# Feed-forward entry: the norm's root moved from the input of three weight units to their outputs

## The chip, the cores and the metric

The kernel runs on one core of a Trainium2 chip. Its metric is the device time in microseconds (us) of one execution; a profile gives in addition the span from the first to the last recorded instruction. Five engines work from queues of their own: TensorE (PE; PEld is its weight load), VectorE (DVE), ScalarE (ACT), GpSimd (POOL) and SyncE (SP, which issues DMAs). Each engine runs its own instructions in the order of the program, and they are tied together by semaphores: an instruction may wait until a counter has reached a value, and raise one when it ends.

## The reference

The reference is a block of two layers on 256 tokens of width 1024, all in float32: a mixer with mixture of experts, and then a second mixer with a feed-forward part. The change lies where the second mixer ends and the feed-forward begins:

```python
for l in range(DEPTH):                      # DEPTH is 1
    u = rmsnorm(h, norm_mix_w[l])
    h = h + hybrid_mixer_2(u, ...)          # ends with merged @ w_o
    v = rmsnorm(h, norm_ffn_w[l])
    h = h + conv_gated_mlp(v, ...)
return rmsnorm(h, final_norm_w)

def rmsnorm(x, w):
    y = x * rsqrt(mean(x * x, axis=-1, keepdims=True) + EPS)
    return y * w

def conv_gated_mlp(v, w_up, ffn_conv_w, ffn_conv_b, w_down):
    h1, h3 = split(v @ w_up, 2, axis=-1)    # w_up is 1024 x 5632
    h1 = causal_dwconv(h1, ffn_conv_w) + ffn_conv_b   # 3 taps along the tokens
    return (silu(h1) * h3) @ w_down
```

The root, rsqrt of a token's mean square, is one number for a token. It multiplies the whole row of the token, so it can be applied to v or to v @ w_up. The convolution mixes tokens, so it has to be in before the taps.

## The kernel before, in words

Tokens stand in two row groups of 128 (t = 0, 1), the width of 1024 in eight groups of 128 (k = 0 to 7). Products in float32 are made of three passes of a shorter float format: each operand is split in a high part (a copy on ScalarE) and a low part (a difference on VectorE), and `product3` issues high by high, high by low and low by high.

The back of the kernel is one stream of weight units through a ring of three slots (`Stream`). SP loads a unit of 1 MB; ScalarE makes its high part (`hi`, line 112, function `split_hi` around it), VectorE its low part (`lo`, line 116, `split_lo`), PE multiplies. A load waits for the low part of the unit three earlier, a high part for the products of the unit three earlier. The second mixer has units 0 to 55, the feed-forward (`ffn`, `BASE` 56) 22 units of up-projection and 12 of down-projection. I call the feed-forward's units 0, 1, 2, ...; the split of unit 57 is that of the feed-forward's unit 1.

The mixer's last four units (52 to 55) multiply the merged rows by `w_o`, two for each half of 512 columns, into banks 4 to 7. VectorE adds them to the hidden rows `s.h` (line 1987, four additions: half c, row group t), each raising `h_done`; between them it makes low parts of units 56 and 57. 

The feed-forward begins with the norm. ScalarE loads the table for logarithm and exponential (line 2222), squares each half of each row group (line 2185), and when the second half of a row group is squared it makes the root (lines 234, 236) and a diagonal matrix of it, `diag` (line 2228). PE multiplies the rows by the diagonal with the rows as its fixed operand (line 2318, 16 products of 128x128, two instructions each), which turns and scales them in one step, into banks 3 to 6. ScalarE copies the turned rows out with the norm's weight as scale (line 2231: `v_hi`), VectorE makes the low parts (line 2266: `v_lo`), and PE starts the first unit as the low parts arrive, k by k.

A unit of the up-projection is 48 products of 128x256 (`features_out`, lines 168 to 170): two feature groups of 128, eight k, three passes, into one of banks 0 to 2. For units 0 to 10 (the convolved half) ScalarE makes the newest tap with the bias (line 2238), then the high part of the unit three later, then Silu (line 2242); VectorE makes the two older taps of both feature groups (line 2276, four instructions), which frees the bank, then the low part of the unit three later. Units 11 to 21 are multiplied by the result.

Of the kernel before, what the change touches and what calls it, by code (L numbers as in the profile page):

```python
# [9 lines left out]
FP32 = mybir.dt.float32  # L10
# [6 lines left out]
P = 128  # L17
T = 256
# [1534 lines left out]
def mixer2(nc, A, s):  # L1553

    XBC_TAPS, A_TAPS, N_HEADS, N_GROUPS = 4, 3, 32, 4
    with ExitStack() as ctx:
# [271 lines left out]
        def vector(dve):  # L1828
# [151 lines left out]
            for c in range(2):  # L1980
                for t in range(TT):
                    if t == 0:
                        dve.wait_ge(out_first, c + 1)
                    else:
                        dve.wait_ge(st.gemm_done, 52 + 2 * c + 2)
                    hc = s.h[:, t, 512 * c:512 * c + 512]
                    dve.tensor_tensor(hc, hc, s.bank[4 + 2 * c + t][:, :], ALU.add).then_inc(h_done, 1)
                split_lo(dve, 56 + c)

        def tensor(pe):  # L1990

# [127 lines left out]
            for n in range(52, 56):  # L2119
                c, kh = O_OUT[n - 52]  # L2120
                pe.wait_ge(st.lo_done, n + 1)
                rows_out(pe, s.bank[4 + 2 * c:6 + 2 * c], st.w(n % 3, 4, 512), 4, lambda part, k: merged_part(part, 4 * kh + k),
                         kh == 0, kh == 1, out_first, st.gemm_done)

        return Programs(sync, gpsimd, scalar, vector, tensor)


def ffn(nc, A, s):
# [5 lines left out]
    with ExitStack() as ctx:  # L2134
# [5 lines left out]
        def sem(name):  # L2140
# [15 lines left out]
            "fw_loaded", "summed", "r_ready", "diag_ready", "vt_mm", "vt_hi", "vt_lo", "tap_done", "h1_ready", "p_ready",  # L2156
            "p_hi_done", "out_first", "act_own", "dve_own", "weighted", "out_ready", "stored"))
        last_scaled = sem("m4_last_scaled")
        h1_flat = h1[:, :, :].rearrange("p a t -> p (a t)")
        squares_of_h = (prod[:, 0, :, :].rearrange("p a t -> p (a t)"), h1_flat[:, 2048:2560])  # L2160
        result = h1_flat[:, 0:2048].rearrange("p (t d) -> p t d", t=TT)
# [17 lines left out]

        def half(x, t, c):  # L2180
            return x[:, t, 512 * c:512 * c + 512]

        def square_half(act, own, i, t, c, done):
            act.wait_ge(done, 2 * c + t + 1)
# [34 lines left out]
        def scalar(act):  # L2219
            own = Count(act, act_own)  # L2220

            act.preload_act_table_set(LOG_EXP)
            for c in range(2):
                for t in range(TT):
                    square_half(act, own, 0, t, c, s.h_done)
                    if c:
                        root_of(act, own, 0, t)
                        act.activation(diag[:, t, :], C("identity"), ACT.Copy, scale=mv[:, t, 4:5]).then_inc(diag_ready, 1)
            for k in range(KD):
                act.wait_ge(vt_mm, k // 2 + 1)  # L2230
                act.activation(v_hi[:, k, :], s.bank[3 + k // 2][:, T * (k % 2):T * (k % 2) + T], ACT.Copy, scale=s.col("norm_ffn_w_2", k)).then_inc(vt_hi, 1)
            split_hi(act, 2)
            for n in range(UP_UNITS):
                act.wait_ge(st.gemm_done, BASE + n + 1)
                if n < UP_UNITS // 2:
                    for t in range(2):
                        f = 2 * n + t
                        act.activation(h1[:, f, :], s.bank[n % 3][:, T * t:T * t + T], ACT.Identity,
                                       scale=s.col("ffn_conv_w_2", KF * (TAPS - 1) + f), bias=s.col("ffn_conv_b_2", f)).then_inc(tap_done, 1)
                    split_hi(act, n + 3)  # L2240
                    act.wait_ge(evac_sem[n % 3], n // 3 + 1)
                    act.activation(pair(h1, n), pair(h1, n), ACT.Silu).then_inc(h1_ready, 1)
                else:
                    c = n - UP_UNITS // 2
                    split_hi(act, n + 3)
                    act.wait_ge(p_ready, c + 1)
                    act.activation(pair(p_hi, c), prod[:, c % 2, :, :].rearrange("p a t -> p (a t)"), ACT.Copy).then_inc(p_hi_done, 1)
            for n in range(UP_UNITS, N_UNITS):
                split_hi(act, n + 3)
            act.preload_act_table_set(LOG_EXP)  # L2250
            for c in range(2):
                for t in range(TT):
                    square_half(act, own, 1, t, c, summed)
                    if c:
                        root_of(act, own, 1, t)
                        act.wait_ge(weighted, 2 * c + t + 1)
                        if t == 0:
                            act.activation(result[:, 0, :], result[:, 0, :], ACT.Copy, scale=mv[:, TT, 4:5]).then_inc(out_ready, 1)
                        else:
                            act.activation(half(result, 1, 1), half(result, 1, 1), ACT.Copy, scale=mv[:, TT + 1, 4:5]).then_inc(out_ready, 1)  # L2260

        def vector(dve):
            own = Count(dve, dve_own)
            for k in range(KD):
                dve.wait_ge(vt_hi, 2 * (k // 2) + 2)
                dve.scalar_tensor_tensor(out=v_lo[:, k, :], in0=s.bank[3 + k // 2][:, T * (k % 2):T * (k % 2) + T], scalar=s.col("norm_ffn_w_2", k),  # L2266
                                         in1=v_hi[:, k, :].bitcast(FP32), op0=ALU.mult, op1=ALU.subtract).then_inc(vt_lo, 1)
            split_lo(dve, 2)
            for n in range(UP_UNITS):
                if n < UP_UNITS // 2:  # L2270
                    dve.wait_ge(tap_done, 2 * n + 2)
                    for d in range(1, TAPS):
                        for t in range(2):
                            f = 2 * n + t
                            o = h1[:, f, d:T]
                            ins = dve.scalar_tensor_tensor(out=o, in0=s.bank[n % 3][:, T * t:T * t + T - d], scalar=s.col("ffn_conv_w_2", KF * (TAPS - 1 - d) + f),
                                                           in1=o, op0=ALU.mult, op1=ALU.add)
                            if d == TAPS - 1 and t == 1:
                                ins.then_inc(evac_sem[n % 3], 1)
# [31 lines left out]
            dve.tensor_scalar(half(result, 1, 0), half(result, 1, 0), mv[:, TT + 1, 4:5], None, op0=ALU.mult).then_inc(last_scaled, 1)  # L2311

        def tensor(pe):
            pe.wait_ge(s.h_done, 3)
            for t in range(TT):
                pe.wait_ge(diag_ready, t + 1)
                for k in range(KD):
                    m = pe.matmul(s.bank[3 + k // 2][:, T * (k % 2) + P * t:T * (k % 2) + P * t + P], lhsT=s.h[:, t, k * P:k * P + P], rhs=diag[:, t, :], start=True, stop=True)
                    if t == 1 and k % 2:
                        m.then_inc(vt_mm, 1)  # L2320
            v = (v_hi, v_lo)

            def up(q, i, used, wait_k=None):
                pe.wait_ge(st.lo_done, q * 3 + i + 1 + BASE)
                if not (isinstance(used, int) and used == 0):
                    pe.wait_ge(evac_sem[i], used)
                features_out(pe, s.bank[i], st.w((BASE + i) % 3, KD, COLS), v, 0, KD, wait_k=wait_k).then_inc(st.gemm_done, 1)

            up(0, 0, 0, lambda k: pe.wait_ge(vt_lo, k + 1))
            for i in range(1, 3):  # L2330
                up(0, i, 0)
            with pe.Fori(1, UP_UNITS // 3) as q:
                for i in range(3):
                    up(q, i, q)
# [181 lines left out]
```

## Time and profile before

| | |
|---|---|
| median of 3 runs | 1704.86 us (1702.92 to 1706.76) |
| profiled execution, its own time | 1705.02 us |
| its span | 1703.2 us |
| PE busy | 1655.8 us, 97% of the span |
| VectorE busy | 676.8 us, 40% |
| ScalarE busy | 577.0 us, 34% |
| mean granted clock of PE | 0.995 of full speed |

Busy time is the time in which an engine had an instruction under way; the chain that ended last is followed back from the last instruction, at each step to what released it. Times within the span are microseconds from its start. A granted clock of 1.00 is PE at full speed, 0.50 at half.

### The profile page before, as it was taken

The numbers are of one execution on the slowest core, as the hardware profiler recorded it, in microseconds if no ns is written. First come the engines' busy times: TensorE is split into PE (matmuls) and PEld (weight loads), VectorE is DVE, ScalarE is ACT, GpSimd is POOL, SyncE is SP. The second block draws the span as 40 slices with busy tenths as digits, with TensorE's granted clock in tenths as the row PEclk, the third lists the DMA queues.
The fourth block names the chain that finished last, engine by engine and source line by source line (L and its number), as shares of the span: only waits on it lengthen the run. The fifth ranks groups of instructions, "written<-read, shape, count | busy, mean of one in ns | idle before, by whom it ended". The sixth has DMA issues, their size and how long they took to land.

```text
span 1703.2 us, 23986 instructions
## 1 busy us (share of the span) xinstructions
PE 1655.8 (97%) x9921; PEld 1053.1 (62%) x9921; DVE 676.8 (40%) x1196; ACT 577.0 (34%) x819; POOL 42.8 (3%) x28
## 2 busy tenths in 40 slices
PE   8999999989999999999999999989999999999998
PEld 8999853333333333333333333349999999989996
DVE  4676641212121211121212121244597565666654
ACT  5655321111111111110111111144464787466433
POOL 0000000000000000000000000000100032000000
PEclk9999999999999999999999999999999999999999
DMA  8556899999999999999999999975555443555552
GB/s 266 199 198 222 303 392 423 428 412 428 431 430 431 431 428 431 429 431 429 432 429 431 428 429 428 431 279 182 181 179 174 149 149 124 177 182 183 187 185 87
DMA packets 150864, 535.15 MB, mean 314 GB/s; under 512 B 7890, under 2 KB 102510, under 8 KB 118030
## 3 DMA queue, kind: packets, MB, share of 16 engines
q1 hardware_dynamic: 150798, 534.20, 79.7%
q8 instruction: 50, 0.82, 0.2%
q14 instruction: 16, 0.13, 0.0%
HBM read 533.13 MB, written 1.05 MB: 314 GB/s over the span
## 4 chain that ended last, share of the span: by engine, by line
PE 62%; DMA 12%; SPq 2%; ACT 1%; DVE 1%; issue 0%; ACTq 0%
PE bank L1434 16%; PE bank L168 10%; PE bank L170 10%; PE bank L169 10%; PE bank L1450 8%; DMA expert_weights<-in_expert_w_up_dram 6%; DMA expert_weights_late<-in_expert_w_up_dram 6%; PE bank L1395 2%; PE bank L1414 2%; PE bank L1441 2%; SPq L1642 1%; PE bank L1403 1%; PE bank L2046 0%; ACT back_w_hi L112 0%; PE bank L1408 0%
## 5 line engine op out<-in xcount | busy, mean ns | idle before, releaser
L1332 DVE TENSOR_TENSOR pre_act<-bank,bias_now 128x512 f32<-128x512 f32 x64 | 44.0, 688 | 655.3 <-PE bank L1441 655.3
L116 DVE TENSOR_TENSOR back_w_lo<-raw_weights,back_w_hi 128x2048 fp32r<-128x2048 f32 x90 | 205.7, 2288 | 91.8 <-ACT back_w_hi L112 90.8
L1434 PE MATMUL bank<-expert_weights_late,x_gathered 128*64 128x512 f32 x1024 | 226.2, 593 | 13.7 <-DMA expert_weights_late<-in_expert_w_up_dram 13.7
L112 ACT ACTIVATE back_w_hi<-raw_weights 128x2048 fp32r<-128x2048 f32 x90 | 170.2, 1892 | 95.1 <-PE bank L170 94.6
L168 PE MATMUL bank<-u_hi,back_w_hi 128*128 128x256 f32 x704 | 200.0, 284 | 0.2 <-DVE u_lo L1838 0.2
L169 PE MATMUL bank<-u_lo,back_w_hi 128*128 128x256 f32 x704 | 199.1, 283 | 0.0
L170 PE MATMUL bank<-u_hi,back_w_lo 128*128 128x256 f32 x704 | 199.1, 283 | 0.0
L1434 PE MATMUL bank<-expert_weights,x_gathered 128*64 128x512 f32 x752 | 167.0, 594 | 8.7 <-DMA expert_weights<-in_expert_w_up_dram 8.7
L1434 PEld LDWEIGHTS bank<-expert_weights_late,x_gathered 128*64 128x64 f32 x1024 | 72.3, 137 | 164.2 <-issue 136.2
L1254 ACT ACTIVATE raw_weights<-bank 128x512 f32<-128x512 f32 x32 | 19.1, 597 | 399.6 <-PE bank L1434 399.6
L168 PEld LDWEIGHTS bank<-u_hi,back_w_hi 128*128 128x128 f32 x704 | 135.0, 192 | 1.0 <-issue 0.7
L169 PEld LDWEIGHTS bank<-u_lo,back_w_hi 128*128 128x128 f32 x704 | 135.0, 192 | 0.0
L170 PEld LDWEIGHTS bank<-u_hi,back_w_lo 128*128 128x128 f32 x704 | 135.0, 192 | 0.0
L1434 PEld LDWEIGHTS bank<-expert_weights,x_gathered 128*64 128x64 f32 x752 | 53.0, 137 | 118.9 <-issue 99.7
L1450 PE MATMUL bank<-expert_weights_late,activations 128*64 128x512 f32 x512 | 113.4, 595 | 0.2 <-DVE activations L1345 0.2
L168 PE MATMUL bank<-v_hi,back_w_hi 128*128 128x256 f32 x352 | 99.9, 284 | 0.2 <-DVE v_lo L2266 0.2
L169 PE MATMUL bank<-v_lo,back_w_hi 128*128 128x256 f32 x352 | 99.6, 283 | 0.0
L170 PE MATMUL bank<-v_hi,back_w_lo 128*128 128x256 f32 x352 | 99.6, 283 | 0.0
L1270 ACT ACTIVATE raw_weights<-bank 128x512 f32<-128x512 f32 x32 | 19.1, 597 | 206.2 <-PE bank L1450 206.2
L1450 PE MATMUL bank<-expert_weights,activations 128*64 128x512 f32 x368 | 82.0, 594 | 0.0
L168 PE MATMUL bank<-x_hi,m_w_hi 128*128 128x256 f32 x272 | 78.1, 287 | 0.0
L169 PE MATMUL bank<-x_lo,m_w_hi 128*128 128x256 f32 x272 | 76.8, 282 | 0.0
(424 smaller groups left out, 2649.9 us busy)
## 6 DMA issues: line engine op xcount, KB each, us to landing
expert_weights_late<-in_expert_w_up_dram SPq DMA_DIRECT2D x64, 2048.0 KB, 25.6
expert_weights<-in_expert_w_up_dram SPq DMA_DIRECT2D x47, 2048.0 KB, 25.3
expert_weights_late<-in_expert_w_down_dram SPq DMA_DIRECT2D x32, 2048.0 KB, 29.2
raw_weights<-in_w_in_dram SPq DMA_DIRECT2D x56, 1024.0 KB, 5.3
expert_weights<-in_expert_w_down_dram SPq DMA_DIRECT2D x23, 2048.0 KB, 28.6
raw_weights<-in_expert_w_up_dram SPq DMA_DIRECT2D x15, 2048.0 KB, 23.8
raw_weights<-in_w_up_dram SPq DMA_DIRECT2D x22, 1024.0 KB, 5.1
raw_weights<-in_expert_w_down_dram SPq DMA_DIRECT2D x8, 2048.0 KB, 28.7
```

Of the source, the lines that this page charges most:

```text
L112: act.activation(self.w_hi[:, s, 0:size], self.s.raw[:, s, 0:size], ACT.Copy).then_inc(self.hi_done, 1)
L116: dve.tensor_tensor(self.w_lo[:, s, 0:size], self.s.raw[:, s, 0:size], self.w_hi[:, s, 0:size].bitcast(FP32), ALU.subtract).then_inc(self. ...
L168: pe.matmul(out, lhsT=ah, rhs=bh, start=start, stop=False, skip_group_check=shared)
L169: pe.matmul(out, lhsT=ah, rhs=bl, start=False, stop=False, skip_group_check=shared)
L170: return pe.matmul(out, lhsT=al, rhs=bh, start=False, stop=stop, skip_group_check=shared)
L1254: act.activation(up_rows[:, 0, :], U[0][:, :], ACT.Copy).then_inc(up_out, 1)
L1332: dve.tensor_tensor(both.rearrange("p g k n -> p (g k) n").rearrange("p a (h n) -> p a h n", h=2), TB[b][:, :].rearrange("p (a h n) -> p a ...
L1395: m = pe.matmul(TB[0][rows[c], :], lhsT=onehot[:, t, :], rhs=s.h[:, t, 512 * c:512 * c + 512], start=(t == 0), stop=(t == 1))
L1414: m = pe.matmul(s.bank[ACC + 2 * t + c][:, :], lhsT=scatter[rows[c], P * t:P * t + P], rhs=y_rows[rows[c], :], start=False, stop=True, ski ...
L1434: m = pe.matmul(U[b][rows[half], :], lhsT=xg[:, 2 * u + a, :], rhs=w[:, a, 512 * c:512 * c + 512], start=(first and a == 0), stop=(last an ...
L1441: m = pe.transpose(TB[b][:, P * gk:P * gk + P], up_rows[:, b, gk:512:4], C("identity"))
L1450: m = pe.matmul(U[0][rows[c], :], lhsT=act_t[:, b, g, half, :], rhs=w[:, half, g, 512 * c:512 * c + 512], start=(b + half + g == 0), stop= ...
```

## The change: what it does

In the new kernel PE turns the unscaled rows by plain transposes, eight behind unit 54 (columns 0 to 511, `turn_h` with c = 0) and eight after the first half of the first feed-forward unit (columns 512 to 1023). ScalarE copies them out with the norm's weight (`raw_high_half`), the first four k between the squares of the two halves and the other four ahead of the squares of the second half; VectorE makes the low parts (`raw_low_half`), the first four k between its low parts of units 56 and 57. These rows lie in memory that the activated products use later.

The first three units use these rows. The first unit is made in two halves of k (`first_up`), with the transposes of the second half of the columns between them. After it, PE multiplies the two diagonals by ones, which gives the roots as a row on every partition; ScalarE copies this to `root_rows`. VectorE multiplies the bank of each of the first three units by it into `prod`, and the taps of these units read `prod` in place of the bank.

The scaled rows for units 3 and later are made beside that: VectorE multiplies the turned rows by weight and root (`rescale`, eight, behind the product of unit 0), ScalarE copies them for the high part (eight, behind the Silu of unit 0), VectorE subtracts for the low part (eight, behind the product of unit 1). PE waits for all eight ahead of unit 3.

The 16 products by the diagonal, and the 8 copies and 8 low parts after them, are gone.

```diff
@@ mixer2, vector @@
-                split_lo(dve, 56 + c)
+                if c == 0:
+                    split_lo(dve, 56)
+                    s.raw_low_half(dve, 0)
+                    split_lo(dve, 57)
@@ mixer2, tensor @@
+                if n == 54:
+                    for t in range(TT):
+                        s.turn_h(pe, t, 0)
@@ ffn @@
+        RAW_UNITS = 3
+        raw_v_hi, raw_v_lo = p_hi[:, 0:KD, :], p_lo[:, 0:KD, :]
+        root_rows = sb("root_rows", [P, T])
+        scaled_v = h1[:, KF - KD:KF, :]
+        def up_of(n, t):
+            return prod[:, n % 2, t, :] if n < RAW_UNITS else s.bank[n % 3][:, T * t:T * t + T]
+        def turned(k):
+            return s.bank[3 + k // 2][:, T * (k % 2):T * (k % 2) + T]
+        def turn_h(pe, t, c):
+            pe.wait_ge(s.h_done, 2 * c + t + 1)
+            for k in range(4 * c, 4 * c + 4):
+                m = pe.transpose(turned(k)[:, P * t:P * t + P], s.h[:, t, k * P:k * P + P], C("identity"))
+            m.then_inc(vt_mm, 1)
+        def raw_high_half(act, c):
+            act.wait_ge(vt_mm, 2 * c + 2)
+            for k in range(4 * c, 4 * c + 4):
+                act.activation(raw_v_hi[:, k, :], turned(k), ACT.Copy, scale=s.col("norm_ffn_w_2", k)).then_inc(vt_hi, 1)
+        def raw_low_half(dve, c):
+            for k in range(4 * c, 4 * c + 4):
+                dve.wait_ge(vt_hi, 2 * (k // 2) + 2)
+                dve.scalar_tensor_tensor(out=raw_v_lo[:, k, :], in0=turned(k), scalar=s.col("norm_ffn_w_2", k),
+                                         in1=raw_v_hi[:, k, :].bitcast(FP32), op0=ALU.mult, op1=ALU.subtract).then_inc(raw_lo, 1)
@@ ffn, scalar @@
             for c in range(2):
+                if c:
+                    raw_high_half(act, c)
                 for t in range(TT):
                     square_half(act, own, 0, t, c, s.h_done)
...
+                if c == 0:
+                    raw_high_half(act, c)
             split_hi(act, 2)
+            act.wait_ge(bc_mm, 1)
+            act.activation(root_rows[:, :], s.bank[7][:, 0:T], ACT.Copy).then_inc(bc_ready, 1)
...
+                    if n < RAW_UNITS:
+                        act.wait_ge(out_scaled, n + 1)
...
                     act.activation(pair(h1, n), pair(h1, n), ACT.Silu).then_inc(h1_ready, 1)
+                    if n == 0:
+                        for k in range(KD):
+                            act.wait_ge(rescaled, k + 1)
+                            act.activation(v_hi[:, k, :], scaled_v[:, k, :], ACT.Copy).then_inc(rescaled_hi, 1)
@@ ffn, vector @@
+            raw_low_half(dve, 1)
             split_lo(dve, 2)
+            dve.wait_ge(bc_ready, 1)
+            def rescale(k):
+                dve.scalar_tensor_tensor(out=scaled_v[:, k, :], in0=turned(k), scalar=s.col("norm_ffn_w_2", k), in1=root_rows[:, :],
+                                         op0=ALU.mult, op1=ALU.mult).then_inc(rescaled, 1)
             for n in range(UP_UNITS):
+                if n < RAW_UNITS:
+                    dve.wait_ge(st.gemm_done, BASE + n + 1)
+                    if n >= 2:
+                        dve.wait_ge(evac_sem[n - 2], 1)
+                    dve.tensor_tensor(prod[:, n % 2, :, :], s.bank[n % 3][:, :].rearrange("p (a t) -> p a t", a=2),
+                                      root_rows[:, :].unsqueeze(1).to_broadcast([P, 2, T]), ALU.mult).then_inc(out_scaled, 1)
+                    if n == 0:
+                        for k in range(KD):
+                            rescale(k)
+                    if n == 1:
+                        for k in range(KD):
+                            dve.wait_ge(rescaled_hi, k + 1)
+                            dve.tensor_tensor(v_lo[:, k, :], scaled_v[:, k, :], v_hi[:, k, :].bitcast(FP32), ALU.subtract).then_inc(vt_lo, 1)
@@ ffn, tensor @@
+            pe.wait_ge(st.lo_done, BASE + 1)
+            first_up(0)
+            for t in range(TT):
+                turn_h(pe, t, 1)
+            first_up(1).then_inc(st.gemm_done, 1)
+            for t in range(TT):
+                pe.wait_ge(diag_ready, t + 1)
+                m = pe.matmul(s.bank[7][:, P * t:P * t + P], lhsT=C("ones"), rhs=diag[:, t, :], start=True, stop=True)
+            m.then_inc(bc_mm, 1)
+            for i in range(1, RAW_UNITS):
+                up(0, i, 0, x=raw_v)
+            pe.wait_ge(vt_lo, KD)
```

`first_up(c)` issues, for both feature groups, the three passes of the four k of half c, each k after its low part (`raw_lo`).

## Rows read from the trace of the kernel before

**Rows 1.** The page, part 1: busy us of each engine, with share and instructions.
```profile
PE 1655.8 (97%) x9921; PEld 1053.1 (62%) x9921; DVE 676.8 (40%) x1196; ACT 577.0 (34%) x819; POOL 42.8 (3%) x28
```
**Rows 2.** Chain that ended last, 1490 to 1510: start, us, what.
```profile
1498.54 1.92 ACT back_w_hi L112
1500.48 1.28 ACT L2222
```
**Rows 3.** Timeline of PE, 1503 to 1510: start, us, line, operation, out<-in.
```profile
1503.27 0.39 PE L169 MATMUL bank<-back_w_lo,ya_hi 128*128 128x512 f32 x1
1503.49 0.39 PE L170 MATMUL bank<-back_w_hi,ya_lo 128*128 128x512 f32 x1
1505.51 3.81 PE L2318 MATMUL bank<-diag,hidden 128*128 128x128 f32 x32 [1.63 <-ACT diag L2228]
1509.52 0.35 PE L168 MATMUL bank<-v_hi,back_w_hi 128*128 128x256 f32 x1 [0.20 <-DVE v_lo L2266]
```
**Rows 4.** Timeline of ScalarE, 1503 to 1522.
```profile
1503.67 0.61 ACT L2185 ACTIVATE h_h<-hidden 128x512 f32<-128x512 f32 x1
...
1504.97 0.40 ACT L2228 ACTIVATE diag<-shared_constants,rms_mv 128x128 f32<-128x128 f32 x1
...
1506.58 0.40 ACT L2228 ACTIVATE diag<-shared_constants,rms_mv 128x128 f32<-128x128 f32 x1
1508.02 3.02 ACT L2231 ACTIVATE v_hi<-bank,parameter_cols 128x256 fp32r<-128x256 f32 x8 [1.04 <-PE bank L2318]
...
1515.71 1.02 ACT L2238 ACTIVATE h<-bank,parameter_cols 128x256 f32<-128x256 f32 x2 [2.86 <-PE bank L170]
...
1521.47 1.02 ACT L2238 ACTIVATE h<-bank,parameter_cols 128x256 f32<-128x256 f32 x2 [0.99 <-PE bank L170]
```
**Rows 5.** Timeline of all engines, 1309 to 1312.5: transposes in the mixer.
```profile
1309.49 1.91 PE L2086 MATMUL bank<-shared_constants,x_b_c 128*128 128x128 f32 x16
...
1310.12 2.48 DVE L1907 TENSOR_TENSOR b_c_v<-bank,dt 128x512 f32<-128x512 f32 x4 [0.43 <-PE bank L2086]
...
1311.15 0.36 PE L168 MATMUL bank<-u_hi,back_w_hi 128*128 128x256 f32 x1
```
**Rows 6.** Timeline of VectorE, 1501 to 1519.
```profile
1501.20 0.69 DVE L1987 TENSOR_TENSOR hidden<-hidden,bank 128x512 f32<-128x512 f32 x1 [3.86 <-PE bank L170]
...
1508.89 3.23 DVE L2266 SCALAR_TENSOR_TENSOR v_lo<-bank,parameter_cols,v_hi 128x256 fp32r<-128x256 f32 x8 [2.08 <-ACT v_hi L2231]
1512.88 2.29 DVE L116 TENSOR_TENSOR back_w_lo<-raw_weights,back_w_hi 128x2048 fp32r<-128x2048 f32 x1 [0.76 <-ACT back_w_hi L112]
1516.76 1.78 DVE L2276 SCALAR_TENSOR_TENSOR h<-bank,parameter_cols,h 128x255 f32<-128x255 f32 x4 [1.59 <-ACT h L2238]
```
**Rows 7.** Groups of VectorE by shape, from 1120: busy us, mean ns, idle before.
```profile
L2290 DVE TENSOR_TENSOR h_h<-bank,h 128x512 f32<-128x512 f32 x11 | 7.6, 692 | 2.8 <-PE bank L170 2.8
...
L1862 DVE TENSOR_SCALAR b_c_v<-b_c_v,parameter_cols 128x256 f32<-128x256 f32 x8 | 2.4, 349 | 0.0
...
L1835 DVE TENSOR_TENSOR w_dt_lo<-w_dt,w_dt_hi 128x256 fp32r<-128x256 f32 x1 | 0.4, 419 | 0.0
```
**Rows 8.** Groups of ScalarE by shape, from 1120.
```profile
L1699 ACT ACTIVATE w_dt_hi<-w_dt 128x256 fp32r<-128x256 f32 x1 | 0.4, 400 | 0.0
```
**Rows 9.** The page, part 6: DMA issues, KB each, median us to landing.
```profile
raw_weights<-in_w_up_dram SPq DMA_DIRECT2D x22, 1024.0 KB, 5.1
```
**Rows 10.** Timeline of PE after two other idle stretches.
```profile
10.40 1.50 PE L963 MATMUL bank<-x_hi,m_w_hi 128*128 128x256 f32 x8 [2.03 <-ACT m_w_hi L449]
...
1140.72 5.46 PE L1998 MATMUL bank<-group_rstd,hidden 128*128 128x128 f32 x32 [2.10 <-DVE hidden L228]
```
**Rows 11.** Windows: us, engines' busy time, then granted clock, DMA share, GB/s.
```profile
12.00:13.00 1.00, 1.00 (x7) 1.00 (x7) 0.74 (x1) 1.00 (x1) 0.00 (x0) 0.50 1.09 387
...
1141.00:1144.30 3.30, 3.30 (x17) 3.30 (x17) 2.28 (x3) 1.75 (x5) 0.10 (x2) 0.50 0.11 13
...
1505.50:1509.40 3.90, 3.81 (x32) 3.63 (x32) 1.82 (x3) 2.76 (x9) 0.00 (x0) 1.00 0.33 91
```

More of the change, by code:

```diff
@@ L2235, in scalar @@
                 if n < UP_UNITS // 2:
+                    if n < RAW_UNITS:
+                        act.wait_ge(out_scaled, n + 1)
                     for t in range(2):
                         f = 2 * n + t
-                        act.activation(h1[:, f, :], s.bank[n % 3][:, T * t:T * t + T], ACT.Identity,
+                        act.activation(h1[:, f, :], up_of(n, t), ACT.Identity,
                                        scale=s.col("ffn_conv_w_2", KF * (TAPS - 1) + f), bias=s.col("ffn_conv_b_2", f)).then_inc(tap_done, 1)
@@ L2275, in vector @@
                             o = h1[:, f, d:T]
-                            ins = dve.scalar_tensor_tensor(out=o, in0=s.bank[n % 3][:, T * t:T * t + T - d], scalar=s.col("ffn_conv_w_2", KF * (TAPS - 1 - d) + f),
+                            ins = dve.scalar_tensor_tensor(out=o, in0=up_of(n, t)[:, 0:T - d], scalar=s.col("ffn_conv_w_2", KF * (TAPS - 1 - d) + f),
                                                            in1=o, op0=ALU.mult, op1=ALU.add)
@@ L2313, in tensor, with up @@
         def tensor(pe):
[L2314 to L2320, printed above, removed]
             v = (v_hi, v_lo)
-            def up(q, i, used, wait_k=None):
+            def up(q, i, used, x=v):
                 pe.wait_ge(st.lo_done, q * 3 + i + 1 + BASE)
@@ L2326, in up, with first_up @@
                     pe.wait_ge(evac_sem[i], used)
[L2327 to L2331, printed above, removed]
+                features_out(pe, s.bank[i], st.w((BASE + i) % 3, KD, COLS), x, 0, KD).then_inc(st.gemm_done, 1)
+            raw_v = (raw_v_hi, raw_v_lo)
+            w = st.w(BASE % 3, KD, COLS)
+            def first_up(c):
+                for t in range(2):
+                    for k in range(4 * c, 4 * c + 4):
+                        pe.wait_ge(raw_lo, k + 1)
+                        f = slice(P * t, P * t + P)
+                        m = product3(pe, s.bank[0][:, T * t:T * t + T], (w[0][:, k, f], w[1][:, k, f]), (raw_v_hi[:, k, :], raw_v_lo[:, k, :]),
+                                     k == 0 and t == 0, k == KD - 1, True)
+                return m
+            pe.wait_ge(st.lo_done, BASE + 1)
[10 more added lines that the diff above has]
+            pe.wait_ge(vt_lo, KD)
             with pe.Fori(1, UP_UNITS // 3) as q:
```

11 lines of the change are left out of this document (4 added, 7 removed).

## The prediction
> **What bounds the kernel now.** I read the page's first part first: TensorE (PE) is busy 1655.8 of 1703.2 us [rows 1]. The change touches one seam, between the mixer's last matmul and the feed-forward's first unit. There the chain of waits [rows 2] leaves PE for the split of weights on ScalarE (ACT) at 1498.54 and an activation table load; squares and roots of both row groups follow there. PE's timeline [rows 3] gives the seam's size. The last mixer matmul starts at 1503.49, 0.22 after the one before, so a next could start at 1503.72; the 16 turning products run from 1505.51; the first unit starts at 1509.52. Units follow each other every 5.76 us (starts of ACT's two rows of evacuations, 1515.71 and 1521.47 [rows 4]). One unit is 48 products, so 0.12 each, and the first takes 5.99 because its first eight k come at VectorE's (DVE) pace. So unit 1 starts at 1515.51 and unit 3 at 1527.03, without a break. With no seam at all unit 1 would start at 1503.72 + 5.76 = 1509.48: the seam holds 6.0 us. That is all the change can win.
>
> **The change, first half.** Eight transposes go behind unit 54. A batch of 16 took 1309.49 to 1311.15 [rows 5], 0.10 each: PE reaches the end of unit 55 at 1503.72 + 0.83 = 1504.55. ACT keeps its order up to the two squares of half 0, so its raw copies of half 0 can begin where the third square began before, at 1503.67 [rows 4]. Copies and low parts before show the hops: copy at 1508.02, low part at 1508.89, product at 1509.52, that is 0.87 and 1.50 after the copy, later copies 0.36 apart (8 in 3.02), low parts 0.39 apart (8 in 3.23, one 0.48) [rows 3, 4, 6]. So low parts run 1504.54 to 1506.20, the first unit's first half starts at 1503.67 + 1.50 = 1505.17 (the late unit 55 is covered by 0.6 us of this wait; without the cover it would cost up to 0.83) and ends after 4 x 0.39 + 12 x 0.12 = 2.97, at 1508.14.
>
> Here a queue turns against the change. DVE is in order: the four low parts wait for ACT, the split of unit 57 stands behind them, and the additions of columns 512 to 1023 behind that. Before, the first of these additions ran at 1501.20 [rows 6]. Now: split 2.29 us from 1506.12 to 1508.41, additions of 0.69 (neighbours overlap by 0.08) to 1509.02 and 1509.63. PE waits for them from 1508.14. From an engine's end to PE is 0.14 (a diagonal ended at 1505.37, its product began at 1505.51 [rows 4, 3]), so the last four transposes start at 1509.77. In the batch before, four transposes released the reader 0.63 after their start (1309.49 to 1310.12) [rows 5]: ACT's copies of half 1 start at 1510.40, PE's second half at 1511.90, ending at 1514.87.
>
> ACT turns to squares and roots of half 1 only after these copies, at 1511.84. From the third square to the second diagonal's end took 1503.67 to 1506.98 [rows 4], 3.31: now 1515.15. PE gets it at 1515.29, adds one product for the root's rows (a pair of instructions, 2 x 0.12 as in the 32 of [rows 3]) and starts unit 1 at 1515.53, against 1515.51. The gain of the first half is nil: 6 us of seam are filled with 5.8 us of new waits.
>
> **The change, second half.** PE needs the scaled rows for unit 3, which it could start at 1515.53 + 2 x 5.76 = 1527.05. What makes them is a DVE queue:
> - ACT's split of unit 58 (1.92 [rows 2], from 1515.06 on) ends at 1516.98, DVE's low part at 1519.30.
> - The product of bank and root row, 128x512, is not in the trace; nearest is a product with a bank at 0.69 [rows 7]: to 1519.91.
> - Eight rescalings have the form of the old low parts (0.48, every 0.39) [rows 6]: to 1523.06.
> - Four taps, 1.78 [rows 6], to 1524.76; ACT's two first taps (1.02 [rows 4]) lie beside the rescalings.
> - The split of unit 59 to 1526.97; the product of unit 1 to 1527.58.
> - Eight subtractions of 128x256, each 0.42 [rows 7], every 0.34: to 1530.30. ACT's Silu after the taps (1.28 of table load [rows 2], and some 0.63, as the squares of its shape take 0.61 [rows 4]) and its eight copies (0.40, at most every 0.36 [rows 8, 4]) are done by 1529.5, beside that.
> So PE starts unit 3 at 1530.44, 3.4 us later than before, after 3.4 idle us. Bounds: if the subtractions cost a full low part (0.48 every 0.39) it is 0.45 more; if all the added operations had the rate of one tensor [rows 7] it is 1.7 less (worked out with the rivals). I take the rows of two tensors, whose form the new ones have.
>
> Behind unit 3 nothing more is late: DVE does the taps of the feed-forward's unit 1 and the split of weight unit 60 by about 1534.2, PE wants that unit at 1536.2, and from there on DVE needs 1.78 + 2.29 of each 5.76. SP's loads wait for low parts, which come up to 7.5 us later; a load takes 5.1 us [rows 9], so that of unit 63, freed by split 60, lands near 1539.3, and ACT asks for it near 1542.
>
> **TensorE's clock.** An idle PE of that length has a second price. PE stood idle 2.03 us before 10.40 and 2.10 us before 1140.72 [rows 10], and both times the granted clock then went from 1.00 to 0.50, the lower of the two levels (1.2 of 2.4 GHz), for some 3 us [rows 11]. After the 1.63 us before 1505.51 it did not [rows 3, 11]. The same 32 turning instructions took 5.46 us in the low stretch and 3.81 at full clock [rows 10, 3]: 1.65 us. The new kernel has PE idle 3.4 us ahead of unit 3, and nearly empty (eight transposes) from 1508.14 to 1511.90, so I expect the low clock in one of the two. Bounds 0 and 1.65; part of it may fall in the idle time itself, so I take 1.3.
>
> The Trainium skill, "TensorE: Matmul & The Clock Gate", section "HAM oscillation — how this bites in real kernels", speaks against this change: long waits between bursts of matmuls let the clock fall, and the next burst starts at the low one. By that rule the sum is 1709.7, without it 1708.4; the trace agrees with the rule at two idle stretches of 2 us.
>
> Sum: 1705.02 us, the profiled execution's own time (span 1703.2 and 1.8 around it), + 3.4 + 1.3 = 1709.7. The median of the runs shown, 1704.86, is 0.16 lower. What this kernel can tell from no change is 0.2%, 3.4 us: the stall alone stands just at that bound.
>
> **The rivals.**
> - Stall without a low clock: 1705.02 + 3.4 = 1708.4. For it: whether the clock falls depends on how the idle stretch lies, and low clock that begins early is spent idle. Against: both idle stretches of 2 us brought it.
> - The other side, not slower than can be told: DVE's added operations run at the faster rate that its operations on one tensor have. A 128x256 of that kind took 0.35 [rows 7], every 0.27: eight rescalings save 1.0, two products at 0.49 save 0.4, so the taps end 1.2 earlier and ACT's copies are done by 1528.3; the subtractions (0.35) then follow these and end at 1528.6. PE starts unit 3 at 1528.7, 1.7 late: 1706.7, with an idle time of 1.7 that by the stretch before 1505.51 leaves the clock alone. It decides from the point where a two-tensor operation of 256 columns takes 0.35 or less. Against: each row with two tensors has the slower rate, 0.42 from SBUF alone among them [rows 7].
> - Low clock in both places: the first delays unit 1 by up to 1.65, which the later stall takes back as it waits for DVE; then the second adds its 1.65 to unit 3, and ACT's taps and splits come late as well. With the upper bound of the subtractions: 1705.02 + 3.4 + 1.65 + 0.45 + some 1 of late ACT work = 1711.5. For it: the first empty stretch is as long as the second.
>
> **How the numbers follow.** Forecast 0.52, stall without low clock 0.27, both places or a longer queue 0.11, the other side 0.10. The forecast is slower by over 3.4 us in all but a few cases, the second case in half of them, the third always: 0.49 + 0.13 + 0.11, less for the scatter of the runs (1702.92 to 1706.76), gives 0.70. Within 0.2%: the other half of the second, nearly all of the other side, 0.24. Faster 0.06: even the other side is no gain, so only what I have not seen gives one. Range 1706.0 to 1712.3: from below the other side, 1706.7, to 0.8 above the third rival.
>
> **What would show it.** Right: the two additions of the second half on DVE after a 2.29 us split, near 1508 to 1510; unit 1 starting within 0.5 us of 1515.5; PE idle some 3.4 us ahead of unit 3 and released by DVE's subtraction; a window at clock 0.5 after either idle stretch. Wrong: unit 1 starting well before 1515, or under 2 us of idle ahead of unit 3, or additions ahead of the split. Then the kernel is not slower by what can be told.

## The result

| | median us | runs | against the kernel before, 95% |
|---|---|---|---|
| before | 1703.51 | 1701.20 to 1706.76 | |
| changed | 1709.05 | 1706.21 to 1711.53 | 1.0034 [1.0027, 1.0042] |
| changed, timed again | 1708.54 | 1707.01 to 1710.43 | 1.0033 [1.0021, 1.0045] |

The change costs 5.5 to 5.6 us. The profiled run of the changed kernel took 1707.76 us, with a span of 1705.9. TensorE's busy time is the same to 1.1 us [rows 1], so nothing shows as saved on it. Where the time went, this number cannot tell, because products at half clock count as busy too.

```profile
PE 1654.7 (97%) x9909; PEld 1052.1 (62%) x9909; DVE 683.9 (40%) x1215; ACT 579.7 (34%) x828; POOL 42.7 (3%) x28
```

One thing must be settled before two profiles of this program are laid side by side. ScalarE's split of unit 57 began at 1498.54 before [rows 2] and begins at 1495.18 here, although the change touches nothing ahead of it. It moves from one execution to the next (1495.18, 1495.56, 1495.01 and 1497.78 in four profiles of the changed kernel). So every time below is a distance from the start of this split. (Read as times within the span, unit 1's start at 1512.04 would be the prediction's sign of being wrong, "well before 1515"; but the split, too, comes 3.36 earlier.) From there to the end of the span it is 1703.2 - 1498.54 = 204.66 us before, and 1705.9 - 1495.18 = 210.72 now: 6.1 longer in this execution.

ScalarE in the changed kernel, timeline 1494 to 1546. The rows answer to [rows 4]: split of unit 57, raw copies of the two halves, second diagonal, first taps of units 0, 3 and 4.

```profile
1495.18 1.92 ACT L112 ACTIVATE back_w_hi<-raw_weights 128x2048 fp32r<-128x2048 f32 x1 [3.52 <-PE bank L170]
...
1500.30 1.55 ACT L2211 ACTIVATE p_hi<-bank,parameter_cols 128x256 fp32r<-128x256 f32 x4
1506.96 1.57 ACT L2211 ACTIVATE p_hi<-bank,parameter_cols 128x256 fp32r<-128x256 f32 x4 [5.11 <-PE bank L2204]
...
1511.35 0.40 ACT L2267 ACTIVATE diag<-shared_constants,rms_mv 128x128 f32<-128x128 f32 x1
...
1516.57 1.09 ACT L2280 ACTIVATE h<-h_h,parameter_cols 128x256 f32<-128x256 f32 x2 [2.75 <-DVE h_h L2323]
...
1535.78 1.02 ACT L2280 ACTIVATE h<-bank,parameter_cols 128x256 f32<-128x256 f32 x2 [0.80 <-PE bank L170]
...
1541.53 1.02 ACT L2280 ACTIVATE h<-bank,parameter_cols 128x256 f32<-128x256 f32 x2 [2.25 <-PE bank L170]
```

VectorE over the same time, for [rows 6]: first the split that stands ahead of the additions, then the queue that makes the scaled rows.

```profile
1502.73 2.28 DVE L116 TENSOR_TENSOR back_w_lo<-raw_weights,back_w_hi 128x2048 fp32r<-128x2048 f32 x1
1504.93 1.28 DVE L1987 TENSOR_TENSOR hidden<-hidden,bank 128x512 f32<-128x512 f32 x2
...
1515.79 0.68 DVE L2323 TENSOR_TENSOR h_h<-bank,root_rows 128x512 f32<-128x512 f32 x1
1516.39 3.22 DVE L2315 SCALAR_TENSOR_TENSOR h<-bank,parameter_cols,root_rows 128x256 f32<-128x256 f32 x8
1519.53 1.78 DVE L2338 SCALAR_TENSOR_TENSOR h<-h_h,parameter_cols,h 128x255 f32<-128x255 f32 x4
1521.23 2.29 DVE L116 TENSOR_TENSOR back_w_lo<-raw_weights,back_w_hi 128x2048 fp32r<-128x2048 f32 x1
1523.43 0.69 DVE L2323 TENSOR_TENSOR h_h<-bank,root_rows 128x512 f32<-128x512 f32 x1
1524.03 2.76 DVE L2331 TENSOR_TENSOR v_lo<-h,v_hi 128x256 fp32r<-128x256 f32 x8
```

TensorE's timeline, for [rows 3]. The brackets hold the idle time and who ended it; 1512.04 is the start of unit 1 and 1527.13 that of unit 3.

```profile
1505.67 1.25 PE L2204 MATMUL bank<-shared_constants,hidden 128*128 128x128 f32 x8 [0.75 <-DVE hidden L1987]
1508.37 0.38 PE L168 MATMUL bank<-p_hi,back_w_hi 128*128 128x256 f32 x1 [1.45 <-DVE p_lo L2216]
...
1512.04 0.36 PE L168 MATMUL bank<-p_hi,back_w_hi 128*128 128x256 f32 x1
...
1527.13 0.55 PE L168 MATMUL bank<-v_hi,back_w_hi 128*128 128x256 f32 x1 [3.33 <-DVE v_lo L2331]
```

Windows around unit 3 (the granted clock is third from the end, as in [rows 11]):

```profile
1526.00:1527.00 1.00, 0.00 (x0) 0.00 (x0) 1.00 (x4) 1.00 (x1) 0.00 (x0) 0.62 1.08 384
1527.00:1533.00 6.00, 5.87 (x27) 5.90 (x28) 4.75 (x8) 2.46 (x5) 0.00 (x0) 0.50 0.56 192
1533.00:1534.00 1.00, 1.00 (x10) 1.00 (x9) 0.96 (x3) 1.00 (x1) 0.00 (x0) 0.97 1.08 385
```

The loss has two terms. Unit 3 would start 1527.03 - 1498.54 = 28.49 us after the split in the kernel before (the prediction's 1527.03); now it starts 31.95 after it, 3.46 late. Unit 4's first tap came at 1538.75 before, 40.21 after the split; now (1541.53) it is 46.35 after it, 6.14 late. So 6.14 - 3.46 = 2.68 us were lost inside unit 3, at half clock. From there on nothing more is lost. The row of the kernel before:

```profile
1538.75 1.02 ACT L2238 ACTIVATE h<-bank,parameter_cols 128x256 f32<-128x256 f32 x2 [2.26 <-PE bank L170]
```

### The profile page after: what moved, and what is told of

It is laid out like the page before. It is cut to its first block, busy times and chain, and to the rows that moved or that the text cites. A ratio compares the mean times of both kernels' runs of the same rounds, so it can differ in the third digit from the quotient of the medians.

```text
span 1705.9 us, 23994 instructions
## 1 busy us (share of the span) xinstructions
PE 1654.7 (97%) x9909; PEld 1052.1 (62%) x9909; DVE 683.9 (40%) x1215; ACT 579.7 (34%) x828; POOL 42.7 (3%) x28
## 4 chain that ended last, share of the span: by engine, by line
PE 62%; DMA 14%; DVE 2%; ACT 1%; issue 1%; SPq 0%; ACTq 0%
PE bank L1434 16%; PE bank L168 10%; PE bank L170 9%; PE bank L169 9%; PE bank L1450 9%; DMA expert_weights_late<-in_expert_w_up_dram 8%; DMA expert_weights<-in_expert_w_up_dram 6%; PE bank L1414 2%; PE bank L1395 2%; PE bank L1441 2%; PE bank L1403 1%; DVE back_w_lo L116 1%; PE bank L2049 0%; ACT back_w_hi L112 0%; PE bank L1408 0%
## 5 line engine op out<-in xcount | busy, mean ns | idle before, releaser
L168 PE MATMUL bank<-v_hi,back_w_hi 128*128 128x256 f32 x304 | 87.4, 288 | 3.3 <-DVE v_lo L2331 3.3
L169 PE MATMUL bank<-v_lo,back_w_hi 128*128 128x256 f32 x304 | 87.3, 287 | 0.0
L170 PE MATMUL bank<-v_hi,back_w_lo 128*128 128x256 f32 x304 | 87.3, 287 | 0.0
```

What stands on the lines that cost most here:

```text
L168: pe.matmul(out, lhsT=ah, rhs=bh, start=start, stop=False, skip_group_check=shared)
L169: pe.matmul(out, lhsT=ah, rhs=bl, start=False, stop=False, skip_group_check=shared)
L170: return pe.matmul(out, lhsT=al, rhs=bh, start=False, stop=stop, skip_group_check=shared)
```

## The experiments

Every kernel is the changed kernel with the edit shown; of long edits the main lines are shown, and `...` stands for lines left out. "Unit 3 start" and "unit 4 late" below are distances from the split of unit 57, set against 28.49 and 40.21.

**The changed kernel again**, timed beside the next two.

> The changed kernel once more, beside the others. Theory (the scaled rows come late from VectorE's queue, PE idles 3.3 us ahead of unit 3, the granted clock then falls): 5 to 6 us above the kernel before, an idle stretch of 3.3 us ahead of unit 3, and the clock at 0.50 behind it for about 3.4 or 6.8 us, which is worth 1.7 to 3 us. Rival (the first half of the change costs time by itself): unit 1 starts over 1 us later after the split of unit 57 on ScalarE than in the kernel before (17.0 us after it there).

Measured: the second line of the first table. Idle 3.34 us, unit 3 at +31.96, unit 4 6.23 late, so the clock took 2.76.

**Fill the idle time.** Three products whose result nobody reads, ahead of the wait for the scaled rows.

```diff
+            pe.wait_ge(bc_ready, 1)
+            for _ in range(3):
+                pe.matmul(s.bank[7][:, :], lhsT=C("identity"), rhs=s.con[:, 1:5, :].rearrange("p n c -> p (n c)"), start=True, stop=True)
             pe.wait_ge(vt_lo, KD)
```

> The changed kernel, with three products of 128x512 by the identity into an unused bank ahead of PE's wait for the scaled rows. Theory: the wait itself stays (unit 3 starts as late), but the clock stays at 1.00 and unit 3 takes 5.8 us in place of 8.6: 2.5 to 3 us less than the changed kernel, 2.5 to 3.3 above the kernel before. Rival (the low clock has another cause than the idle time, or costs less than it seems): within 1 us of the changed kernel.

Measured: 1705.91 us, 1.0021 [1.0012, 1.0031] of before, 2.6 less than the changed kernel beside it (1708.54). TensorE's timeline, with the added products:

```profile
1524.29 2.74 PE L2409 MATMUL bank<-shared_constants 128*128 128x512 f32 x6
1527.80 0.35 PE L168 MATMUL bank<-v_hi,back_w_hi 128*128 128x256 f32 x1 [0.78 <-DVE v_lo L2331]
```

The window over them and unit 3:

```profile
1524.00:1540.00 16.00, 15.22 (x112) 13.47 (x112) 14.59 (x26) 11.68 (x17) 0.00 (x0) 1.00 0.57 192
```

Unit 3 starts at 1527.80 - 1495.84 = 31.96, no sooner than without the filling, and the clock stays at 1.00. What goes is only the second term; what stays is the stall (the profile's end is 208.16 after the split, 3.50 later than before). This splits the loss into its two parts.

**Additions ahead of the split of unit 57** on VectorE, which tests the queue that the prediction names in the first half.

```diff
                     s.raw_low_half(dve, 0)
-                    split_lo(dve, 57)
+            split_lo(dve, 57)
```

> The changed kernel, with VectorE's two additions of the second half ahead of the low part of unit 57. Theory: everything from the second transposes on comes 1.0 us earlier, the idle stretch ahead of unit 3 stays as long, so 1.0 us less than the changed kernel, 4 to 5 above the kernel before. Rival (the queue ahead of the additions is not what holds the second half): no change, within 0.4 us.

Measured: 1706.79 us, 1.0020 [1.0011, 1.0029]; 1.75 less than the changed kernel, and 3.9 above the kernel before beside it (1702.92), a little less than forecast. The second raw copies begin 1508.27 - 1497.60 = 10.67 after the split of unit 57 instead of 11.78, and unit 3 starts at 30.85 instead of 31.95: the 1.1 us run through to unit 3. The end of this profile is 1706.1 - 1497.60 = 208.50 after the split against 210.72; the other 1.1 is a shorter stretch of low clock (below). The idle time ahead of unit 3 does not shrink, because the queue that makes the scaled rows moves with unit 0:

```profile
1528.45 0.36 PE L168 MATMUL bank<-v_hi,back_w_hi 128*128 128x256 f32 x1 [3.34 <-DVE v_lo L2331]
```

**Raw copies first.** ScalarE makes the raw copies of half 0 ahead of the table load and the two squares.

```diff
+            raw_high_half(act, 0)
             act.preload_act_table_set(LOG_EXP)
...
-                if c == 0:
-                    raw_high_half(act, c)
```

> The changed kernel, with ScalarE's four raw copies of half 0 ahead of its table load and squares. Theory (the first half gains nothing because ScalarE and VectorE come to it late): copies 3.2 us earlier, VectorE's additions done as PE ends unit 55, the second copies 2.2 us earlier, unit 1 about 2 us earlier against the split of unit 57; the idle stretch of 3.3 us ahead of unit 3 stays: 1.7 to 2.3 us less than the changed kernel, 3 to 4 above the kernel before. Rival (ScalarE's order is covered by other waits): within 0.5 us of the changed kernel.

Measured: 1706.06 us, 1.0015 [1.0006, 1.0024]; 3.1 above the kernel before beside it (1702.96), as forecast. ScalarE's timeline:

```profile
1498.61 1.92 ACT L112 ACTIVATE back_w_hi<-raw_weights 128x2048 fp32r<-128x2048 f32 x1 [3.52 <-PE bank L170]
1500.43 1.55 ACT L2211 ACTIVATE p_hi<-bank,parameter_cols 128x256 fp32r<-128x256 f32 x4
...
1508.64 1.57 ACT L2211 ACTIVATE p_hi<-bank,parameter_cols 128x256 fp32r<-128x256 f32 x4 [3.35 <-PE bank L2204]
```

The first copies come 1.82 after the split's start instead of 5.12, the second 10.03 instead of 11.78, and unit 3 starts at 1528.82 - 1498.61 = 30.21, 1.74 sooner. Of the two faults of the first half, each taken away alone, the place of the copies was the dearer; the two edits together, with nothing else, were not run. The idle time is again 3.34:

```profile
1528.82 0.35 PE L168 MATMUL bank<-v_hi,back_w_hi 128*128 128x256 f32 x1 [3.34 <-DVE v_lo L2330]
```

**The root at all outputs.** All 22 units take the raw rows; nothing is rescaled. Units 11 to 21 get a further product on VectorE.

```diff
-        RAW_UNITS = 3
-        raw_v_hi, raw_v_lo = p_hi[:, 0:KD, :], p_lo[:, 0:KD, :]
+        RAW_UNITS = UP_UNITS // 2
+        raw_v_hi, raw_v_lo = v_hi, v_lo
...
-                    if n == 0:
-                        for k in range(KD):
-                            rescale(k)
...
-            pe.wait_ge(vt_lo, KD)
...
+                    own.add(dve.tensor_tensor(pr, s.bank[n % 3][:, :], pair(h1, c), ALU.mult))
+                    own.wait()
+                    dve.tensor_tensor(prod[:, c % 2, :, :], prod[:, c % 2, :, :],
+                                      root_rows[:, :].unsqueeze(1).to_broadcast([P, 2, T]), ALU.mult).then_inc(p_ready, 1)
```

> All 22 units of the up-projection use the unscaled rows, and VectorE applies the root to each unit's output (units 11 to 21 with one product more): the eight rescalings, eight copies and eight subtractions are gone, the first half of the change stays as it is. Theory: no idle time ahead of unit 3 and no low clock, so 5 to 6 us less than the changed kernel, within 1 us of the kernel before (the first half gains nothing). Rival (the extra products on VectorE bind): 0.2 us or more for each of 11 units, 2.5 us and more above the kernel before.

Measured: 1704.15 us, 1.0003 [0.9994, 1.0012]; 1.2 above the median of the kernel before beside it (1702.96), 0.5 by the ratio. There is no idle time ahead of unit 3, so the rescaling is the whole of the stall. But the first half on its own earns nothing either. In this profile the clock fell in the first sparse stretch instead, and unit 1 starts at 1515.01 - 1497.18 = 17.83, 0.86 later than before; the end (1702.7 - 1497.18 = 205.52) is later by the same 0.86:

```profile
1509.00:1510.00 1.00, 0.00 (x0) 0.00 (x0) 0.16 (x1) 1.00 (x3) 0.00 (x0) 0.98 1.07 380
1510.00:1511.00 1.00, 0.62 (x3) 0.62 (x4) 1.00 (x3) 1.00 (x4) 0.00 (x0) 0.50 1.04 358
1511.00:1512.00 1.00, 1.00 (x6) 1.00 (x6) 0.50 (x2) 0.90 (x5) 0.00 (x0) 0.50 0.36 124
```

**Interleaved.** The root at all outputs, copies first, and the first two units each in two halves of k: unit 1's first half stands between the late transposes and unit 0's second half. Splits 58 and 59 stand ahead of the row of roots (`root_rows`), and VectorE starts its taps one by one.

```diff
...
-            first_up(1).then_inc(st.gemm_done, 1)
+            pe.wait_ge(st.lo_done, BASE + 2)
+            half_up(1, 0)
+            half_up(0, 1).then_inc(st.gemm_done, 1)
+            half_up(1, 1).then_inc(st.gemm_done, 1)
...
```

> All units on unscaled rows, raw copies of half 0 first, the first two units each in two halves of k with unit 1's first half between the transposes and unit 0's second half, high and low parts of units 58 and 59 ahead of the roots, taps started one by one. Theory (the seam of 6 us can be filled if no engine waits in it): unit 2 starts 4 us earlier after the split of unit 57 than in the kernel before, no low clock: 3 to 4.3 us less than the kernel before. Rival (VectorE's backlog of products, taps and splits holds the later units): the gain at unit 2 is given back by unit 10, within 1 us of the kernel before.

Measured: 1701.37 us, 0.9988 [0.9979, 0.9997]. The trace lists no wait of TensorE in the stretch, and unit 2 starts 1515.41 - 1496.59 = 18.82 after the split of unit 57 (22.73 before: 28.49 - 5.76). That is 3.9 us won, as forecast, but only 204.66 - 202.61 = 2.05 reach the end, less than the 3 to 4.3 expected; about half was given back, as the rival has it. ScalarE's splits stand 5.99 apart, TensorE's unit takes 5.76, and from 1538 on TensorE's products show gaps of 0.22 to 0.27 at the start of each unit, some 0.23 a unit given back. The start of unit 2 and two of the splits:

```profile
1515.41 0.36 PE L168 MATMUL bank<-v_hi,back_w_hi 128*128 128x256 f32 x1
...
1528.24 1.90 ACT L112 ACTIVATE back_w_hi<-raw_weights 128x2048 fp32r<-128x2048 f32 x1
...
1534.23 1.90 ACT L112 ACTIVATE back_w_hi<-raw_weights 128x2048 fp32r<-128x2048 f32 x1
```

The cycle goes round two engines: product (VectorE), first taps and split (ScalarE), low part (VectorE), and the next product stands behind that low part in VectorE's queue.

**High parts first.** The interleaved kernel, with the split ahead of the two first taps.

```diff
+                    if n:
+                        split_hi(act, n + 3)
...
                     for t in range(2):
...
-                    if n:
-                        split_hi(act, n + 3)
```

> The interleaved kernel with all units on unscaled rows, and ScalarE's high part of the unit three later ahead of its two first taps in units 1 to 10. Theory (product, first taps, high part and low part in a row, 5.99 us, are the chain that took back 1.9 us of the 3.9 us won at unit 2): high parts follow each other every 5.76 us, the 3.9 us stay: 3.4 to 4 us less than the kernel before, 1.5 to 2 less than the interleaved kernel. Rival (VectorE's added products themselves bind): cycle stays at 5.9 us or more, as the interleaved kernel.

Measured: 1700.11 us, 0.9978 [0.9969, 0.9987]: 3.1 us faster than the kernel before, and the best of all. The splits now stand 5.36 apart, less than TensorE's 5.76, and one wait is left, 0.5 us for the low part of weight unit 60 ahead of unit 4. The end comes 1703.1 - 1501.58 = 201.52 after the split, 3.14 sooner than before, a little short of the 3.4 to 4 expected.

```profile
1536.35 1.90 ACT L112 ACTIVATE back_w_hi<-raw_weights 128x2048 fp32r<-128x2048 f32 x1
...
1541.71 1.90 ACT L112 ACTIVATE back_w_hi<-raw_weights 128x2048 fp32r<-128x2048 f32 x1
```

**Four raw units** in place of three.

```diff
-        RAW_UNITS = 3
+        RAW_UNITS = 4
...
-            for i in range(1, RAW_UNITS):
+            for i in range(1, 3):
                 up(0, i, 0, x=raw_v)
+            up(1, 0, 1, x=raw_v)
...
```

> The changed kernel with four units on unscaled rows in place of three, everything else as it is. Theory (the stall is the scaled rows' lateness, 3.3 us, against a unit of 5.76): PE needs them one unit later and finds them; what is late next is the low part of weight unit 60, 1.4 us after PE could start the fourth unit (1530.7 against 1529.3 in the changed kernel's times), and the clock stays: 4 to 5 us less than the changed kernel, 0.5 to 2 above the kernel before. Rival (the units on unscaled rows are slow by themselves): no less than the changed kernel.

Measured: 1704.21 us, 1.0003 [0.9994, 1.0012]. The scaled rows are now in time: the last subtraction ends at 1526.90 + 2.76 = 1529.66. A shorter wait of 1.21 us stands ahead of unit 4, and the clock stays at 1.00 through it. The profile names no releaser for it, but VectorE's low part of weight unit 60 ends at 1533.56, 0.10 ahead of unit 4's first product, as the theory had it. In the rows, VectorE's low parts of units 60, 61 and 62, each with the first product of its unit behind it:

```profile
1531.28 2.28 DVE L116 TENSOR_TENSOR back_w_lo<-raw_weights,back_w_hi 128x2048 fp32r<-128x2048 f32 x1
...
1533.66 0.36 PE L168 MATMUL bank<-v_hi,back_w_hi 128*128 128x256 f32 x1 [1.21 <-issue]
...
1537.26 2.29 DVE L116 TENSOR_TENSOR back_w_lo<-raw_weights,back_w_hi 128x2048 fp32r<-128x2048 f32 x1
...
1539.61 0.38 PE L168 MATMUL bank<-v_hi,back_w_hi 128*128 128x256 f32 x1
...
1543.25 2.29 DVE L116 TENSOR_TENSOR back_w_lo<-raw_weights,back_w_hi 128x2048 fp32r<-128x2048 f32 x1
...
1545.60 0.39 PE L168 MATMUL bank<-v_hi,back_w_hi 128*128 128x256 f32 x1
```

Unit 4 starts 1533.66 - 1498.04 = 35.62 after the split of unit 57, 1.37 later than before, and the end comes 1.8 later. The last 0.4 lies at units 5 and 6: they start 5.95 and 5.99 after the unit ahead of them in place of 5.76, each 0.06 behind the end of the low part of its weights, and these low parts stand 5.98 and 5.99 apart.

**How long is the clock low?** The changed kernel's two profiles lost 2.7 us to it, those of the two kernels with an earlier start 1.55 each. Two more profiles of the changed kernel and two of the one with the additions first were to tell whether that follows from the kernel (A) or differs between executions (B).

> The changed kernel once more, for a third profile of its low clock. Its two profiles so far show 2.7 us lost in unit 3 to a low stretch of some 7 us, the kernels with unit 1 started earlier 1.55 us to one of some 3.5. Theory A, the length follows from where the idle time lies in the kernel: again 2.6 to 2.8 us, clock 0.50 for 6 to 7 us from before unit 3's start. Theory B, it differs from execution to execution, as the clock after the 2.10 us idle near 1140 does: sooner or later a profile of this kernel with 1.5 us or none. Idle of 3.3 us ahead of unit 3 in both.

> The changed kernel, a fourth profile. A: unit 3 loses 2.6 to 2.8 us, low for 6 to 7 us. B: 0, 1.5 or 2.7, not the same as in the third.

> The kernel with the split of unit 57 behind the additions, a second profile. A: unit 3 again loses 1.5 to 1.6 us, low for some 3.5 us. B: the loss is another, up to 2.7 or none. The second half's copies at +10.67 us from the split of unit 57 and the 3.3 us idle in both.

> The same kernel, a third profile. A: 1.5 to 1.6 us, low for some 3.5 us. B: another loss than in the second.

Measured, in the way of the result's two terms (in the third profile ScalarE was itself late for unit 4's tap, so that of unit 5 is taken):

| profile | idle ahead of unit 3 | unit 3 start | lost to the low clock behind it |
|---|---|---|---|
| changed, first | 3.33 | +31.95 | 2.68 |
| changed, again | 3.34 | +31.96 | 2.76 |
| changed, third | 2.12 | +31.95 | 0.07 |
| changed, fourth | 3.34 | +31.96 | 1.56 |
| additions first, three profiles | 3.34 each | +30.85, +30.83, +30.83 | 1.55, 1.55, 1.57 |

Windows of the third profile of the changed kernel: the clock was low behind the sparse stretch of the first half, as unit 0's second half and unit 1's start ran, and full around unit 3. The late unit 1 used up 1.2 us of the idle time ahead of unit 3.

```profile
1509.00:1512.00 3.00, 3.00 (x16) 3.00 (x16) 0.32 (x1) 2.84 (x9) 0.00 (x0) 0.50 0.08 27
...
1526.00:1534.00 8.00, 7.04 (x59) 7.07 (x60) 6.70 (x12) 4.45 (x5) 0.00 (x0) 1.00 0.70 237
```

Windows of the fourth: low from 1530.0 to 1533.5 only, where the first was low from 1526.2 to 1533.0.

```profile
1530.00:1531.00 1.00, 1.00 (x7) 1.00 (x7) 0.96 (x3) 0.00 (x0) 0.00 (x0) 0.52 1.12 402
1531.00:1533.00 2.00, 2.00 (x11) 2.00 (x11) 2.00 (x2) 0.63 (x1) 0.00 (x0) 0.50 0.40 156
```

For the changed kernel A falls: one and the same program, with unit 3 starting at the same distance to 0.01 us, lost 0.1, 1.6, 2.7 and 2.8. What decides it within an execution stays open; so does why the kernel with the additions first lost nearly the same, 1.55 to 1.57, three times out of three.

## Why the prediction was right, and which term was off

The mechanism held: the two waits stand where the forecast put them, and each of its steps was met within 0.2 us. That the total came within 0.7 us of the median is in part luck, as the last two terms show. In distances from the split of unit 57 (the forecast's times less 1498.54, the trace's less 1495.18):

| step | forecast | trace |
|---|---|---|
| raw copies of half 0 begin | 5.13 | 5.12 |
| second addition of half 1 ends | 11.09 | 11.03 |
| raw copies of half 1 begin | 11.86 | 11.78 |
| second diagonal ends | 16.61 | 16.57 |
| unit 1 starts | 16.99 | 16.86 |
| last subtraction ends | 31.76 | 31.61 |
| unit 3 starts | 31.90 | 31.95 |

- **First half: nil, as forecast.** Unit 1 starts 0.1 sooner than before (16.97). The split ahead of the additions is there on VectorE, 2.28 us and then the two additions, and taking it away gives 1.1 us back. The prediction named that queue as what turns against the change. The place of the first copies behind the table load and squares, which it took as given, was the other fault: 1.74 us.
- **Second half: the stall, as forecast.** Idle 3.33 us against 3.4, released by VectorE's subtraction. Rescalings at 3.22 for eight and the product at 0.68 have the two-tensor durations that the prediction took; the subtractions stand 0.34 apart, as it had them. With no scaled rows to wait for (the root at all outputs) the wait is gone, and with four raw units the scaled rows come in time; the 1.21 us there is a wait for weights. One step beside the path was off without effect: the sum puts ScalarE's table load behind the taps, while in the trace the load runs ahead of their end, so that the eight copies are done 29.25 after the split in place of 30.96.
- **The mis-sized term is the low clock.** The step reads "Bounds 0 and 1.65; part of it may fall in the idle time itself, so I take 1.3". Its bound came from one low stretch, of some 3.4 us, that 32 turning products saw [rows 10, 11]. In the first profile of the changed kernel the clock was low for 6.8 us, twice as long, and 5.9 of them lay in unit 3; in the fourth it was low for 3.5. The term measured 2.68, 2.76, 0.07 and 1.56: a mean of 1.8, and an upper end well above the bound. Both low stretches that the prediction had were some 3 us long; what it mis-sized is how long the clock stays low. In the first, 28 products start every 0.21 us (1527.13 to 1533.04) instead of every 0.12, which makes 2.5 of the 2.68. With 3.46 of stall the sum is 5.2, against 5.5 and 5.6 in the medians; the forecast's 3.4 + 1.3 was 4.7.
- **The distance to the median hides this.** The forecast started from an execution of 1705.02, 1.5 above the median of all runs (1703.51). That execution had itself met the low clock near 1140, worth 1.2 us (last section). Too high a start and too small a loss leave 1709.7 beside 1709.05, which is luck: the added time was forecast at 4.7 and is 5.5.
- **"Both idle stretches of 2 us brought it" was a sample of one execution.** The clock stayed full at the second of these places in the changed kernel's first profile, after the same 2.10 us of idle time, and the 32 products took 4.23 us, not 5.46:

```profile
1138.60 4.23 PE L2001 MATMUL bank<-group_rstd,hidden 128*128 128x128 f32 x32 [2.10 <-DVE hidden L228]
```

The rivals: the stall without a low clock is what filling the idle time makes, +3.0 us, and what one of four executions of the changed kernel did by itself. There the low clock came in the first stretch, delayed unit 1, and was taken back by the wait for VectorE, as the third rival has it for the first place; both places in one execution was not seen. The other side, VectorE's faster rate, is out: its durations are those of two tensors. On the rule of the Trainium skill's "TensorE: Matmul & The Clock Gate", section "HAM oscillation — how this bites in real kernels", the runs agree that a wait can let the clock fall and that the products behind it then run at the low one. The third execution, at full clock behind an idle time of 2.12 us, and the row above, at full clock behind 2.10, say that a wait of two microseconds need not. In the filled kernel's profile the clock stayed at 1.00.

## What to carry to other kernels

When a scale is moved from a matmul's input to its output, write down the queue of the engine that now makes the late copy, in its order: here the gain at the front was eaten by one split and one table load ahead of short urgent work, and the loss behind it was VectorE's queue, not TensorE's arithmetic. Of the kernels tried, moving the scale paid in two. In both no scaled copy was made at all, the raw copies came first, and TensorE had another half unit to work on during the hand-over (2.0 us won at the end); in the second the split also stood ahead of the taps, so that the two-engine cycle (5.36 us) was shorter than TensorE's unit (5.76), and 3.1 us were won. No scaled copy alone won nothing; interleaving with a scaled copy was not tried. A stall of TensorE has a second price in the clock; read it from several executions and give it a wide range (here from 0.1 to 2.8 us behind a stall of 2.1 to 3.3, up to about half of the unit behind it).

## What the hardware showed that I had not expected

- The same idle time at the same place lets the clock fall in one execution and not in the next. Ahead of the 32 turning products near 1140 TensorE was idle for 2.1 to 3.3 us in all 14 profiles of this study; the clock then fell in 5 of them (one after 2.98 us, four after 2.09 or 2.10) and stayed full in 9 (among them one after 3.30 us).
- These falls are a part of why the work ahead of the seam ends at different times (the split of unit 57 begins between 1493.34 and 1501.58 in the 14 profiles): a low clock near 1140 alone cost 5.46 - 4.23 = 1.2 us.
